# One 512-column matmul on hi|lo activations in place of two of 256, in a split-float32 GEMM chain

## The chip, the core and the metric

The program runs on one core of one Trainium2 chip. The metric is the device time of one execution in microseconds, from the first to the last instruction; the median of several runs is quoted. In this kernel TensorE (PE) multiplies into PSUM, ScalarE (ACT) and VectorE (DVE) read PSUM and SBUF, GpSimd (POOL) works on SBUF, SyncE (SP) issues the weight transfers.

## What is computed

Two transformer-like blocks over 256 tokens of width 2048, all in float32. First block: RMS norm, an input projection, attention over three dilations (8 heads), a diagonal state-space mixer with a gated unit, an output projection, and a gated FFN of 5632. Second block: one wide input projection, a two-way linear recurrence (LRU), local attention, attention over a memory, three gated branches merged and projected, and an FFN of 8192 with squared ReLU.

```
hn = rmsnorm(h, norm1);  q, k, v, u = split(hn @ w_in)
h  = h + concat([attention(q, k, v), ssm(u)]) @ w_out
hn = rmsnorm(h, norm2);  h = h + (silu(hn @ w_gate) * (hn @ w_up)) @ w_down
x  = rmsnorm(h, final)
xr, gr, q, k, v, qm, gl = split(rmsnorm(x, pre) @ w_in_2)
merged = sum over 3 branches of sigmoid(gl_n + b) * (y_n @ w_br_n)
x  = x + rmsnorm(merged @ w_out_2)
x  = x + rmsnorm(relu(rmsnorm(x) @ w_up)^2 @ w_down)
```

Nearly all the work is products of activations [256 x K] with weights [K x N].

## The kernel before

**Numbers.** The matmuls take f32r, which the kernel uses as a float32 of fewer bits. So each operand is split into a high part, its f32r rounding, and a low part, the rest; a product a*w is taken as ah*wh + al*wh + ah*wl, three f32r matmuls into the same PSUM address.

**Tiling.** The activations lie transposed, 128 features x 256 tokens a tile, 16 tiles; XH, XL and UH, UL are the split parts of two operand buffers, each a tensor of its own. A GEMM is a chain of *bodies* (138 in the program); a body has 8 *slots*, and makes 512 output features: slots 0 to 3 are the four quarters of K for the first 256 outputs, slots 4 to 7 for the second 256. A slot is one transfer of weights (512 KB where K is 2048) into RAW, a ring of 4 buffers. In `units` a slot has 2 x kt triples of matmuls (kt is 4, in three stages 2 and in one 3): n picks 128 output features, k the 128 rows of K; each result is 128 x 256 and lies in the first half (0:T) of a bank of 512 floats. Outputs 0 and 1 of the half body p use banks 2p and 2p+1 of `gemm_psum`. In a few stages (`tokens_out`) the activations are the stationary operand and 256 weight columns stream.

**Who feeds whom.** For each slot ScalarE (`upper`, L688) waits for the transfer and for TensorE to have left the ring buffer (mm_done of four slots earlier), and rounds RAW into HI. VectorE (`lower`, L1104) subtracts into LO and counts up lo_done, which TensorE waits for before the slot, and the queue of SyncE before it loads the buffer again. At a half body's first slot TensorE also waits for evac[p], which says that banks 2p and 2p+1 have been read.

**Order.** ScalarE and VectorE both run `stream`: at slot j of a body they first split slot j's weights and then do the *event* of slot j-3 (LAG = 3). The events of slots 3 and 7 hold the evacuation of a finished half body: on VectorE `taken` waits for mm_done and gives the view of the two banks, and the operation that follows (scaling by the norm, an addition to the residual) reads PSUM and counts evac[p]. In the gated unit (glu) ScalarE takes the sigmoid from PSUM itself. The other events are attention, state space, recurrence and so on; their small matmuls stand between TensorE's slots and use the other four banks. What an engine waits for in an event holds back the next slot's split too, because each queue is in order.

The residual stages (`residual`, L1373 in the output projection of the state-space part, L1368 in the last down projection of the first block) have the longest event: VectorE adds, multiplies by the next gain (L1375), waits for ScalarE's rounding into XH, and subtracts into XL (L1377); ScalarE waits for L1375 before it rounds.

## Time and profile before

| | before |
|---|---|
| median of 3 runs | 3399.64 us (3398.23 to 3400.7) |
| span of the profiled execution | 3399.2 us |
| TensorE busy | 3279.3 us, 96% |
| VectorE busy | 2136.7 us, 63% |
| ScalarE busy | 1530.1 us, 45% |
| GpSimd busy | 532.6 us, 16% |
| read from HBM | 571.13 MB |

A busy matmul row is as long as the matmul takes from its start to its modelled end; the next one begins long before that, so a group's busy figure is not its share of the time. The share is to be taken from a stretch without gaps, by the count of its matmuls.

### The profile page before, as it was taken

Reading aid. Unit: us, or ns where it says so; the run is one execution under the profiler, and the core shown is the slowest. Engines: PE = TensorE matmul, PEld = TensorE weight load, DVE = VectorE, ACT = ScalarE, POOL = GpSimd, SP = SyncE. Lnnn points to the kernel's source line nnn. Section 1 sums busy time; section 2 is a strip of 40 time slices with the busy share of each in tenths; the row PEclk is TensorE's granted clock in tenths of the full one; section 3 lists DMA queues with packets and bytes.
Section 4 is the critical chain, followed back from the end, with each engine's and each line's share of the span. In section 5 each row is a group of like instructions: output and inputs, shape, how many; then the busy total and the mean of one; then the engine's idle time right before and its main releaser. Section 6 shows DMA issues by size and latency. Waiting matters only on the chain.

```text
span 3399.2 us, 67239 instructions
## 1 busy us (share of the span) xinstructions
PE 3279.3 (96%) x26280; PEld 3212.2 (94%) x26280; DVE 2136.7 (63%) x2409; ACT 1530.1 (45%) x1885; POOL 532.6 (16%) x511
## 2 busy tenths in 40 slices
PE   5999999999999999899999999999997999999997
PEld 5898889999999999899999999999997999999997
DVE  7788887755555555857865666455556655555555
ACT  3444445454334344337753556444333333333342
POOL 5343443300000000703430000000014000000002
PEclk9999999999999999999999999999998999999999
DMA  6444444655555555555555444555553455555553
GB/s 212 151 154 147 156 142 143 193 184 167 194 184 180 176 182 171 162 193 173 167 195 179 154 149 161 178 174 174 181 173 118 161 186 178 187 180 186 180 185 124
DMA packets 169036, 580.49 MB, mean 171 GB/s; under 512 B 19072, under 2 KB 20864, under 8 KB 168896
## 3 DMA queue, kind: packets, MB, share of 16 engines
q1 hardware_dynamic: 160272, 558.16, 49.8%
q0 software_dynamic: 3408, 10.75, 0.9%
q10 hardware_dynamic: 5216, 9.64, 0.8%
q8 instruction: 97, 1.59, 0.2%
q14 instruction: 43, 0.35, 0.0%
HBM read 571.13 MB, written 7.34 MB: 170 GB/s over the span
## 4 chain that ended last, share of the span: by engine, by line
PE 87%; DVE 9%; issue 2%; ACT 2%; DMA 0%; ACTq 0%; DVEq 0%; POOL 0%; POOLq 0%; SPq 0%
PE gemm_psum L326 26%; PE gemm_psum L327 26%; PE gemm_psum L328 26%; DVE weights_lo L1104 3%; PE gemm_psum L320 1%; PE gemm_psum L321 1%; PE gemm_psum L322 1%; PE bank_b L338 1%; ACT weights_hi L688 1%; DVE projections L1375 0%; DVE x_lo L1127 0%; PE bank_s L570 0%; PE bank_b L591 0%; PE bank_s L602 0%; DVE late L1217 0%
## 5 line engine op out<-in xcount | busy, mean ns | idle before, releaser
L1104 DVE TENSOR_TENSOR weights_lo<-weights,weights_hi 128x1024 fp32r<-128x1024 f32 (+2 forms) x1104 | 1349.9, 1236 | 968.6 <-ACT weights_hi L688 962.6
L688 ACT ACTIVATE weights_hi<-weights 128x1024 fp32r<-128x1024 f32 (+2 forms) x1104 | 1109.9, 1018 | 1427.0 <-PE gemm_psum L328 1262.3
L326 PE MATMUL gemm_psum<-x_hi,weights_hi 128*128 128x256 f32 x5120 | 1467.4, 287 | 68.3 <-DVE weights_lo L1104 41.7
L327 PE MATMUL gemm_psum<-x_lo,weights_hi 128*128 128x256 f32 x5120 | 1455.9, 284 | 0.0
L328 PE MATMUL gemm_psum<-x_hi,weights_lo 128*128 128x256 f32 x5120 | 1455.5, 284 | 0.0
L326 PEld LDWEIGHTS gemm_psum<-x_hi,weights_hi 128*128 128x128 f32 x5120 | 985.2, 192 | 81.0 <-issue 37.4
L327 PEld LDWEIGHTS gemm_psum<-x_lo,weights_hi 128*128 128x128 f32 x5120 | 985.3, 192 | 0.8
L328 PEld LDWEIGHTS gemm_psum<-x_hi,weights_lo 128*128 128x128 f32 x5120 | 985.1, 192 | 0.0
L326 PE MATMUL gemm_psum<-u_hi,weights_hi 128*128 128x256 f32 x2880 | 826.0, 287 | 17.6 <-DVE weights_lo L1104 15.2
L327 PE MATMUL gemm_psum<-u_lo,weights_hi 128*128 128x256 f32 x2880 | 816.2, 283 | 0.0
L328 PE MATMUL gemm_psum<-u_hi,weights_lo 128*128 128x256 f32 x2880 | 816.1, 283 | 0.0
L326 PEld LDWEIGHTS gemm_psum<-u_hi,weights_hi 128*128 128x128 f32 x2880 | 549.2, 191 | 24.1 <-DVE weights_lo L1104 15.8
L327 PEld LDWEIGHTS gemm_psum<-u_lo,weights_hi 128*128 128x128 f32 x2880 | 549.2, 191 | 1.0
L328 PEld LDWEIGHTS gemm_psum<-u_hi,weights_lo 128*128 128x128 f32 x2880 | 549.1, 191 | 0.0
L1886 POOL TENSOR_TENSOR work<-projections 128x512 f32 x16 | 26.4, 1649 | 956.3 <-DVE projections L1696 698.0
L1803 POOL TENSOR_TENSOR work<-projections 128x512 f32<-128x512 f32 x8 | 12.3, 1539 | 711.8 <-DVE projections L1368 711.8
L1872 POOL DMA_DIRECT2D work<-memk_scratch x8 | 4.3, 536 | 500.1 <-ACT late L1002 364.7
L320 PE MATMUL gemm_psum<-weights_hi,u_hi 128*128 128x256 f32 x256 | 75.3, 294 | 0.0
L321 PE MATMUL gemm_psum<-weights_hi,u_lo 128*128 128x256 f32 x256 | 72.4, 283 | 0.0
L322 PE MATMUL gemm_psum<-weights_lo,u_hi 128*128 128x256 f32 x256 | 72.3, 283 | 0.0
L1083 ACT ACTIVATE u_hi<-work 128x512 f32 (+1 forms) x32 | 20.2, 632 | 109.5 <-DVE work L1682 109.5
L1780 POOL TENSOR_TENSOR late<-late 128x256 f32<-128x256 f32 x32 | 31.0, 970 | 154.0 <-DVE late L1221 154.0
(338 smaller groups left out, 2553.6 us busy)
## 6 DMA issues: line engine op xcount, KB each, us to landing
weights<-in_w_branch SPq DMA_DIRECT2D x192, 512.0 KB, 3.3
weights<-in_w_gu SPq DMA_DIRECT2D x176, 512.0 KB, 3.4
weights<-in_w_up SPq DMA_DIRECT2D x128, 512.0 KB, 3.5
weights<-in_w_down SPq DMA_DIRECT2D x128, 512.0 KB, 3.3
weights<-in_w_dn SPq DMA_DIRECT2D x64, 512.0 KB, 3.3
weights<-in_w_in_qk SPq DMA_DIRECT2D x32, 512.0 KB, 3.3
weights<-in_w_mem_k SPq DMA_DIRECT2D x32, 512.0 KB, 3.5
weights<-in_w_mem_v SPq DMA_DIRECT2D x32, 512.0 KB, 3.4
```

Of the source, the lines that this page charges most:

```text
L320: pe.matmul(o, ah, wh, start=first, stop=False)
L321: pe.matmul(o, al, wh, start=False, stop=False)
L322: mm = pe.matmul(o, ah, wl, start=False, stop=end)
L326: pe.matmul(o, wh, xh[:, kk, :], start=first, stop=False)
L327: pe.matmul(o, wh, xl[:, kk, :], start=False, stop=False)
L328: mm = pe.matmul(o, wl, xh[:, kk, :], start=False, stop=end)
L338: mm = pe.matmul(bank_b[:, n, :], b_stage[rows, n, :], u_stage[rows, :], start=True, stop=True)
L688: act.activation(HI[:, j % RING, 0:g.kt * GC], RAW[:, j % RING, 0:g.kt * GC], ACT.Copy)\
L1083: act.activation(UH[:, ix(b(4, 2 * (slot // 4)), 2), :], up_space, ACT.Copy).then_inc(up_hi, 1)
L1104: dve.tensor_tensor(LO[:, j % RING, cols], RAW[:, j % RING, cols], HI[:, j % RING, cols].bitcast(f32), ALU.subtract).then_inc(lo_done, 1)
L1780: pool.tensor_tensor(state_h[:, 0, :], prod_c[:, 0, :], prod_s[:, 1, :], ALU.add)
L1886: pool.tensor_tensor(squares[:, 0:2, :], t, t, ALU.mult).then_inc(sq_step, 1)
```

## The change

HI and LO become the two planes of one tensor WS (`weights_split`), XH and XL those of XS (`x_split`, 512 floats a tile: high | low), UH and UL those of US. In `units` one matmul with the high weights streams both planes of the activations, 512 columns, into the whole bank (`both`); a second, with the low weights, streams the high plane into the first half. In the `tokens_out` stages the high activations stand still and high | low weights stream. So a result now lies in two halves of a bank that must be added.

No VectorE operation reads both halves: ScalarE copies the second half of both banks to SBUF (`staged`, tensor `halves`, one buffer for each p), at the head of the events of slots 3 and 7, after waits for mm_done and for evac[p] of the body before. `taken` on VectorE waits for that copy (half_out) in place of mm_done, adds the first half onto it, counts `summed`, waits for it, and hands on the buffer in SBUF; the operation that used to read PSUM reads SBUF, and counts evac[p] as before. In glu, VectorE makes the sum too and ScalarE's sigmoid waits for it. After the last stage ScalarE does the events that were left over (slots 5 to 7), which it did not need to before.

```
-                            pe.matmul(o, wh, xh[:, kk, :], start=first, stop=False)
-                            pe.matmul(o, wh, xl[:, kk, :], start=False, stop=False)
-                            mm = pe.matmul(o, wl, xh[:, kk, :], start=False, stop=end)
+                            pe.matmul(both, HI[:, j % RING, cols], xs[:, kk, :, :], start=first, stop=False)
+                            mm = pe.matmul(o, LO[:, j % RING, cols], xs[:, kk, 0, :], start=False, stop=end)
...
+            def staged(g, events):
+
+                def f(slot, b):
+                    if slot in (3, 7):
+                        p = slot // 4
+                        wait(act, mm_done, b(SLOTS, SLOTS * g.first + slot + 1))
+                        wait(act, evac[p], b(1, g.first))
+                        act.activation(halves[p], GP[:, 2 * p:2 * p + 2, T:2 * T], ACT.Copy).then_inc(half_out, 1)
+                    events(slot, b)
+                return f
...
             def taken(g, b, slot):
 
-                wait(dve, mm_done, b(SLOTS, SLOTS * g.first + slot + 1))
-                return GP[:, 2 * (slot // 4):2 * (slot // 4) + 2, 0:T]
+                p = slot // 4
+                wait(dve, half_out, b(2, 2 * g.first + p + 1))
+                dve.tensor_tensor(halves[p], halves[p], GP[:, 2 * p:2 * p + 2, 0:T], ALU.add).then_inc(summed, 1)
+                wait(dve, summed, b(2, 2 * g.first + p + 1))
+                return halves[p]
...
-                    act.wait_ge(mm_done, SLOTS * (glu.first + b()) + slot + 1)
+                    act.wait_ge(summed, 2 * (glu.first + b()) + slot // 4 + 1)
...
+            for slot in range(SLOTS - LAG, SLOTS):
+                late[0](slot, late[1])
```

The order of the instructions on TensorE, in the first slot of the program, before:

```order
L326 MATMUL gemm_psum<-x_hi,weights_hi 128x256 [waits lo_done,xl_done]
L327 MATMUL gemm_psum<-x_lo,weights_hi 128x256
L328 MATMUL gemm_psum<-x_hi,weights_lo 128x256
L326 MATMUL gemm_psum<-x_hi,weights_hi 128x256
L327 MATMUL gemm_psum<-x_lo,weights_hi 128x256
L328 MATMUL gemm_psum<-x_hi,weights_lo 128x256
```

and with the change (L326 and L327 are lines of the changed kernel):

```order
L326 MATMUL gemm_psum<-x_split,weights_split 128x512 [waits lo_done,xl_done]
L327 MATMUL gemm_psum<-x_split,weights_split 128x256
L326 MATMUL gemm_psum<-x_split,weights_split 128x512
L327 MATMUL gemm_psum<-x_split,weights_split 128x256
L326 MATMUL gemm_psum<-x_split,weights_split 128x512
```

Each triple has become a pair; nothing else moved there.

On VectorE, the first evacuation of the output projection of the state-space part, before:

```order
L1104 TENSOR_TENSOR weights_lo<-weights,weights_hi 128x512 [waits hi_done] x4
L1373 TENSOR_TENSOR residual<-residual,gemm_psum 128x512 [waits mm_done]
L1375 TENSOR_TENSOR projections<-residual,vecs 128x512 [waits evac0]
L1377 TENSOR_TENSOR x_lo<-projections,x_hi 128x512 [waits res_hi]
L1104 TENSOR_TENSOR weights_lo<-weights,weights_hi 128x512 [waits hi_done]
```

and with the change (L1116 is the weights' low part, L1123 the addition in `taken`, L1390 the residual):

```order
L1116 TENSOR_TENSOR weights_split<-weights,weights_split 128x512 [waits hi_done] x4
L1123 TENSOR_TENSOR halves<-halves,gemm_psum 128x512 [waits half_out]
L1390 TENSOR_TENSOR residual<-residual,halves 128x512 [waits summed]
L1392 TENSOR_TENSOR projections<-residual,vecs 128x512 [waits evac0]
L1394 TENSOR_TENSOR x_split<-projections,x_split 128x2x256 [waits res_hi]
L1116 TENSOR_TENSOR weights_split<-weights,weights_split 128x512 [waits hi_done]
```

One operation more stands ahead of the residual, and two waits, for ScalarE's copy and for the sum.

On ScalarE, at the same place, with the change (before, the row of L697 is not there; L687 rounds the weights, L876 the activations):

```order
L687 ACTIVATE weights_split<-weights 128x512 [waits mm_done,raw_in1]
L687 ACTIVATE weights_split<-weights 128x512 [waits mm_done,raw_in2]
L697 ACTIVATE halves<-gemm_psum 128x512 [waits evac0,mm_done]
L876 ACTIVATE x_split<-projections 128x2x256 [waits res_g]
L687 ACTIVATE weights_split<-weights 128x512 [waits mm_done,raw_in3]
```

The copy stands between the rounding of slot 6's weights and that of slot 7's.

## Rows read from the trace of the kernel before

**Rows 1.** The page: busy time and share, then the granted clock in 40 slices.

```profile
PE 3279.3 (96%) x26280; PEld 3212.2 (94%) x26280; DVE 2136.7 (63%) x2409; ACT 1530.1 (45%) x1885; POOL 532.6 (16%) x511
...
PEclk9999999999999999999999999999998999999999
```

**Rows 2.** The page: the chain that ended last, by line.

```profile
PE gemm_psum L326 26%; PE gemm_psum L327 26%; PE gemm_psum L328 26%; DVE weights_lo L1104 3%; PE gemm_psum L320 1%; PE gemm_psum L321 1%; PE gemm_psum L322 1%; PE bank_b L338 1%; ACT weights_hi L688 1%; DVE projections L1375 0%; DVE x_lo L1127 0%; PE bank_s L570 0%; PE bank_b L591 0%; PE bank_s L602 0%; DVE late L1217 0%
```

**Rows 3.** Groups by line: busy us, mean ns of one, idle time before them.

```profile
L326 PE MATMUL gemm_psum<-x_hi,weights_hi 128*128 128x256 f32 x5120 | 1467.4, 287 | 68.3 <-DVE weights_lo L1104 41.7
L327 PE MATMUL gemm_psum<-x_lo,weights_hi 128*128 128x256 f32 x5120 | 1455.9, 284 | 0.0
...
L326 PE MATMUL gemm_psum<-u_hi,weights_hi 128*128 128x256 f32 x2880 | 826.0, 287 | 17.6 <-DVE weights_lo L1104 15.2
```

**Rows 4.** Stretches: length, busy us (count) of each engine, clock, DMA share, GB/s.

```profile
265.60:394.80 129.20, 125.99 (x900) 113.25 (x899) 107.94 (x142) 61.53 (x86) 51.71 (x54) 0.99 0.47 149
...
601.90:654.80 52.90, 48.04 (x387) 46.44 (x385) 43.04 (x55) 24.27 (x41) 25.99 (x21) 1.00 0.54 169
...
1352.10:1431.30 79.20, 70.85 (x578) 69.43 (x577) 68.24 (x62) 29.52 (x40) 51.49 (x49) 1.00 0.48 155
...
1527.00:1632.90 105.90, 105.90 (x834) 104.23 (x834) 77.00 (x97) 83.94 (x120) 43.66 (x36) 1.00 0.52 169
...
2916.90:3009.00 92.10, 92.10 (x770) 92.10 (x769) 46.04 (x42) 34.38 (x33) 0.00 (x0) 1.00 0.56 183
```

**Rows 5.** Timeline of TensorE: start us, length us, what.

```profile
3000.03 0.28 PE L326 MATMUL gemm_psum<-u_hi,weights_hi 128*128 128x256 f32 x1
3000.04 0.19 PEld L327 LDWEIGHTS gemm_psum<-u_lo,weights_hi 128*128 128x128 f32 x1
3000.15 0.28 PE L327 MATMUL gemm_psum<-u_lo,weights_hi 128*128 128x256 f32 x1
```

**Rows 6.** Chain in order of time, and timeline: other matmuls.

```profile
2123.65 3.46 PE bank_s L602 x16
...
1444.19 0.95 PE L532 MATMUL bank_a<-ones,squares 128*128 128x1 f32 x8
1444.98 0.19 PEld L326 LDWEIGHTS gemm_psum<-x_hi,weights_hi 128*128 128x128 f32 x1
```

**Rows 7.** A stretch at the lower clock, and two matmuls in it.

```profile
2625.70:2628.30 2.60, 2.20 (x11) 1.91 (x9) 2.60 (x3) 1.71 (x4) 2.01 (x1) 0.50 0.00 0
...
2626.21 0.41 PE L328 MATMUL gemm_psum<-x_hi,weights_lo 128*128 128x256 f32 x1
2626.42 0.41 PE L326 MATMUL gemm_psum<-x_hi,weights_hi 128*128 128x256 f32 x1
```

**Rows 8.** Timeline of one slot's two weight splits, in brackets idle before.

```profile
3003.53 1.06 ACT L688 ACTIVATE weights_hi<-weights 128x1024 fp32r<-128x1024 f32 x1 [1.82 <-PE gemm_psum L328]
...
3004.63 1.23 DVE L1104 TENSOR_TENSOR weights_lo<-weights,weights_hi 128x1024 fp32r<-128x1024 f32 x1 [1.66 <-ACT weights_hi L688]
```

**Rows 9.** Timeline of half a body of the state-space output projection.

```profile
626.92 0.39 PE L326 MATMUL gemm_psum<-u_hi,weights_hi 128*128 128x256 f32 x1 [0.51 <-DVE weights_lo L1104]
...
629.13 0.68 DVE L1373 TENSOR_TENSOR residual<-residual,gemm_psum 128x512 f32 x1
629.96 0.69 DVE L1375 TENSOR_TENSOR projections<-residual,vecs 128x512 f32 x1
630.80 0.63 ACT L866 ACTIVATE x_hi<-projections 128x512 f32 x1 [3.71 <-DVE projections L1375]
631.58 0.69 DVE L1377 TENSOR_TENSOR x_lo<-projections,x_hi 128x512 f32 x1 [0.92 <-ACT x_hi L866]
...
633.48 0.38 PE L326 MATMUL gemm_psum<-u_hi,weights_hi 128*128 128x256 f32 x1 [0.55 <-DVE weights_lo L1104]
```

**Rows 10.** Groups by line, shapes kept apart: a PSUM copy, a PSUM addition, a self-wait.

```profile
L776 ACT ACTIVATE work<-bank_s 128x512 f32<-128x512 f32 x8 | 4.6, 580 | 0.0
...
L1696 DVE TENSOR_TENSOR projections<-projections,gemm_psum 128x512 f32 x18 | 12.4, 688 | 12.4 <-PE gemm_psum L328 12.4
...
L1492 DVE SCALAR_TENSOR_TENSOR work<-projections,vecs,work 128x255 f32<-128x255 f32 x16 | 7.8, 484 | 2.4 <-DVE work L1490 2.3
```

More of the change, by code:

```diff
@@ L165, in program @@
         consts = sb("consts", [P, 4])
+        HS = sb("halves", [P, 2, 2 * T])
+        halves = [HS[:, n, :].rearrange("p (a t) -> p a t", a=2) for n in range(2)]
         def vec(name, a=0, n=None):
@@ L250, in program @@
         hi_done, lo_done, mm_done = sem("hi_done"), sem("lo_done"), sem("mm_done")
+        half_out, summed = sem("half_out"), sem("summed")
         angle_in, theta_done, angle_done, bbar_done = sem("angle_in"), sem("theta_done"), sem("angle_done"), sem("bbar_done")
@@ L858, in glu_events @@
                        .then_inc(gh_done, 1)
-            late = stream(act, glu, upper, late, glu_events, tail=gelu_y)
+            late = stream(act, glu, upper, late, staged(glu, glu_events), tail=gelu_y)
             def out_ssm_events(slot, b):
@@ L866, in out_ssm_events @@
                     act.activation(XH[:, ix(tiles, 2), :], ZP[:, 0:2, :], ACT.Copy).then_inc(res_hi, 1)
-            late = stream(act, out_ssm, upper, late, out_ssm_events)
+            late = stream(act, out_ssm, upper, late, staged(out_ssm, out_ssm_events))
             act.wait_ge(ol_done, H1)
@@ L904, in _ @@
             for n, (up, down) in enumerate(ffn1):
-                late = stream(act, up, upper, late, up_events(up, done))
+                late = stream(act, up, upper, late, staged(up, up_events(up, done)))
                 done += up.bodies
-                late = stream(act, down, upper, late, last_down_events if n == 2 else nothing,
+                late = stream(act, down, upper, late, staged(down, last_down_events if n == 2 else nothing),
                               tail=(second_constants, lru_constants, None)[n])
@@ L1061, in branch_events @@
                 return f
-            late = stream(act, branches[0], upper, late, branch_events(0))
-            late = stream(act, branches[1], upper, late, branch_events(1), tail=operand(0, q_late, UH))
-            late = stream(act, branches[2], upper, late, branch_events(2), tail=operand(1, qm, UH))
-            late = stream(act, out2, upper, late, nothing, tail=operand(2, merged, XH))
+            late = stream(act, branches[0], upper, late, staged(branches[0], branch_events(0)))
+            late = stream(act, branches[1], upper, late, staged(branches[1], branch_events(1)), tail=operand(0, q_late, UH))
+            late = stream(act, branches[2], upper, late, staged(branches[2], branch_events(2)), tail=operand(1, qm, UH))
+            late = stream(act, out2, upper, late, staged(out2, nothing), tail=operand(2, merged, XH))
             def mixed():
@@ L1086, in _ @@
             for n, (up, down) in enumerate(ffn2):
-                late = stream(act, up, upper, late, up2_events(8 * n), tail=mixed if n == 0 else None)
-                late = stream(act, down, upper, late, nothing)
+                late = stream(act, up, upper, late, staged(up, up2_events(8 * n)), tail=mixed if n == 0 else None)
+                late = stream(act, down, upper, late, staged(down, nothing))
+            for slot in range(SLOTS - LAG, SLOTS):
+                late[0](slot, late[1])
             root(7, bank_y[:, 0, :], rms[:, 1, :])
@@ L1350, in glu_events @@
             def glu_events(slot, b):
+                if slot in (3, 7):
+                    taken(glu, b, slot)
                 if slot == 7:
```

55 lines of the change are left out of this document (26 added, 29 removed).

## The prediction

> **What bounds the kernel now.** Read the page first. TensorE is busy 96% of a span of 3399.2 us at a mean granted clock of 0.99 of the 2.4 GHz level, and the next engine, VectorE, 63% [rows 1]. The chain that ended last lies on TensorE for 87%, in three lines of equal weight, the three matmuls of one product [rows 2]. The groups by line say what these are: 128x128 weights over 256 columns, a busy figure of 284 to 287 ns each [rows 3]. These overlap, so the price of one is not its row but its share of a stretch. The stretch from 2916.9 to 3009.0 is one down projection of the second block, 4 bodies of 8 slots of 24 matmuls = 768, in 92.1 us: **120.0 ns each**, 2.88 us a slot, with no gap [rows 4]. At 2.4 GHz 256 columns last 106.7 ns, so each matmul pays 13.3 ns on top of its columns. The program has 138 bodies, 1104 slots, and 8448 such triples (5120+2880+256+192 by the counts in the groups by line), together 8448 x 360 ns = 3041 us of the 3399.
>
> The change leaves the columns as they are (512+256 = 3x256) and takes away one instruction, one weight load, of each triple. So the question is what the 13.3 ns belong to: to each matmul, to its weight load, or to its columns.
>
> **The matmuls.** Three places of the trace bear on it. (1) A stream of plain f32 matmuls at 2.4 GHz, 16 records in 3.46 us, 216 ns each [rows 6]: L602 has 8 matmuls there and 16 records, each of which passes its 256 columns twice (512 column times, 213.3 ns) and each has a full weight load of its own. There the extra is 3 ns, and a load is hidden under 512 column times. (2) Where the clock stood at 1.2 GHz (granted 0.50), our own matmuls start 0.21 us apart [rows 7], 256/1.2 = 213 ns: nothing on top. (3) Eight matmuls of a single column, each with a full load: after the first, seven loads between 1444.19 and 1444.98, 0.113 us each [rows 6]. So a load alone repeats in 113 ns, less than our 120, and in our stream the next load starts 0.01 us after the matmul does [rows 5]: it would be through before the 120 ns are over. The load alone does not explain the 13.3 ns; something at the start of each full-rate matmul with a load beside it does, and it vanishes when the columns go at half rate, as in (1) and (2).
>
> I take it as **fixed for each matmul**: the 512-column one costs 213.3+13.3 = 226.7 ns, the pair 346.7 against 360.0, a gain of 13.3 ns a triple. Bounds: 216+120 = 336 ns if the wide matmul behaves as in (1) (gain 24), and 240+120 = 360 if the extra goes with the columns (gain 0). A stream of 512 full-rate columns does not occur before the change, so no row is nearer; the middle value is also the one between the bounds, and (1) and (2) show that what exists is not a share of every column in every mode.
>
> By the Trainium skill ("TensorE: Matmul & The Clock Gate", section "Back-to-back issue gap") a matmul takes its columns over 2.4 GHz plus 2.5 ns; by that the triple would cost 328 and the pair 325 ns, a gain of 3 ns, and the change would lose more than it wins. The trace has 120 ns where that rule gives 109, and agrees with it only in the f32 stream; the time by that rule would fall beside the third rival below.
>
> Two stages don't give this gain, since TensorE waits for VectorE in them: the output projection of the state-space part (601.9 to 654.8, VectorE busy 43.0 of 52.9 us) and the last down projection of the first block (1352.1 to 1431.3, 68.2 of 79.2) [rows 4]. They hold 128 and 192 triples. So 8128 triples x 13.3 ns = **-108 us** (bounds -193 and 0).
>
> **The evacuations.** Each body has two, 276 in all. Added: on ScalarE a copy of 128x512 from PSUM, 0.58 us by the row of the same shape; on VectorE an addition of 128x512 with one operand in PSUM, 0.69 us, and its wait for itself, 0.15 us as where an operation reads what the one before wrote [rows 10]. That is 0.84 us of VectorE and 0.6 of ScalarE each, 232 and 160 us over the run. VectorE's wait is now for half_out, which stands behind ScalarE's split of slot 6 (or 2 of the next body); behind it on VectorE are the event's arithmetic and the low part of the next slot's weights, and TensorE waits for that. What covers it: ScalarE rounds a slot's weights as soon as TensorE has left the ring's buffer, with three slots still to go before that slot. Its row starts at 3003.53, VectorE's low part ends at 3005.86 [rows 8], 2.33 us after the release, and TensorE starts on it three slots = 8.64 us after the release: 6.3 us in hand. With the change three slots last 8.3 us and the chain grows by 0.6+0.84 and less than 1 us of queueing: still over 3 us. **Nothing** in stages of that kind.
>
> Where the cover is thin:
> - The output projection of the state-space part. A half body takes 6.56 us (TensorE's stalls end at 626.92 and 633.48) against 5.76 of matmuls, and VectorE runs through all of it: addition, gain, a wait for ScalarE's high part, low part, four weight splits [rows 9]. The copy can start before VectorE comes (the matmuls of slot 7 end at about 628.4, VectorE adds at 629.13), so only VectorE's own 0.84 us counts: 8 x 0.84 = **+7 us** (up to 8 x 1.45 = 12).
> - The last down projection of the first block has the same shape and less lead: 8 x (0.84 to 1.45) = **+9 us** (7 to 12).
> - Where a stage can't start before the last evacuation of the one before (into the first block's FFN, into the second block, into its MLP, and the end) the chain grows by 0.6+0.84 = 1.45 us: 4 x 1.45 = **+6 us**.
> - The recurrent stages (ScalarE 83.9 and VectorE 77.0 of 105.9 us) and the state-space stages before 577 (VectorE 107.9 of 129.2, 84%) [rows 4]. A body of 32.3 us there has 27.0 of VectorE's work; it becomes 28.7 of 31.4 us (91%) and stays under TensorE's time, but chains through both engines are long. Nothing at best, 60 us if a third of the added VectorE time there shows; I take **+15 us**.
>
> Sum on the profiled execution: 3399.2 - 108 + 7 + 9 + 6 + 15 = 3328. The span lies 0.4 us under the median of the runs, 3399.64, which is inside their own spread (3398.2 to 3400.7). **Forecast 3330 us.**
>
> **The rivals.**
> - *The weight load is what binds* 256-column matmuls, and a wide one hides it: 336 ns a pair. For it: the load alone already takes 113 of the 120 ns, and the f32 stream pays 3 ns. Against: the next load's row starts with the matmul's own. The gain is 193 us, and as TensorE outruns the splits sooner I take 40 for the costs: 3245 us. The Trainium skill gives a load its columns over 1.2 GHz (same page, section "LDWEIGHTS"), 107 ns for 128 columns, which would put the 256-column matmul right at that edge; the trace agrees within 6 ns.
> - *Half fixed, half by columns*: 233+120 = 353 ns, a gain of 6.7 x 8128 = 54 us; 3399 - 54 + 37 = 3382 us.
> - *By columns alone*, the slower side: reading 4-byte columns at 2.4 GHz is what falls short, 240 ns for 512. For it: the extra is absent exactly where columns go at half rate. Then the gain is 0 and the 37 us of evacuations stay: 3436 us. It decides from a wide matmul of 235.5 ns on, where 8128 x 4.6 ns just pay the 37.
> - *The evacuations hurt more*: the two halves run through three engines in order, and in the state-space and recurrent stages VectorE becomes the bound. With the fixed price, -108 + 22 + 60 = 3373 us.
>
> **How the numbers follow.** Fixed price 0.42, load-bound 0.14, half and half 0.18, by columns 0.18, costly evacuations 0.08. The range from 3240 to 3408 leaves out the case by columns and little else. A measurement of this kernel can tell about 0.2% (7 us) from no change. Faster by more than that: 0.40 + 0.14 + 0.13 + 0.06 = 0.73; within it 0.07; slower 0.20.
>
> **What would show it.** In a down projection of the second block, a slot of 8 pairs: 2.77 us if fixed, 2.69 if load-bound, 2.88 if by columns (92.1 us for the stage becomes 88.7, 86.1 or stays). Copy rows of some 0.58 us x276 on ScalarE and additions of 0.69 us x276 on VectorE. In the two VectorE-bound stages, 60 and 88 us instead of 52.9 and 79.2. TensorE's waits for weights_lo outside these and the stage starts should stay near zero; if they spread over the state-space stages, my 15 us are too few. The forecast is wrong in kind if the slot stays at 2.88 us.

## The result, and the profile after

The changed kernel takes **3420.76 us** (median of 6 runs, 3407.51 to 3430.6) against 3399.18 (6 runs, 3397.82 to 3400.7): ratio 1.006, 95% interval 1.0042 to 1.0078. That is 21.6 us slower, where 3330 was forecast and 3240 to 3408 was the range. The profiled execution is one of 3427.63 us with a span of 3425.9.

The page of the changed kernel: busy time, and the chain that ended last by line.

```profile
PE 3237.2 (94%) x17832; PEld 2763.8 (81%) x17832; DVE 2312.3 (67%) x2685; ACT 1672.8 (49%) x2161; POOL 534.8 (16%) x511
...
PE 77%; DVE 14%; ACT 5%; issue 3%; ACTq 0%; DVEq 0%; DMA 0%; POOL 0%; POOLq 0%; SPq 0%
```

8448 matmuls and their loads are gone, and TensorE's busy time fell by only 42 us (3279.3 in [rows 1]). 10 points of the chain have moved from TensorE to VectorE, ScalarE and issue (it was 87% TensorE): TensorE waits more. Its waits for the weights' low parts grew from 56.9 us in all to 93.4.

Groups of the changed kernel, by line (busy us, mean ns of one, idle before them):

```profile
L326 PE MATMUL gemm_psum<-x_split,weights_split 128*128 128x512 f32 x5120 | 1837.9, 402 | 88.0 <-DVE weights_split L1116 61.1
L327 PE MATMUL gemm_psum<-x_split,weights_split 128*128 128x256 f32 x5120 | 1444.7, 282 | 0.0
...
L697 ACT ACTIVATE halves<-gemm_psum 128x512 f32<-128x512 f32 x276 | 164.9, 597 | 522.9 <-PE gemm_psum L327 504.8
L1123 DVE TENSOR_TENSOR halves<-halves,gemm_psum 128x512 f32<-128x512 f32 x276 | 189.2, 686 | 274.9 <-ACT halves L697 273.6
```

They answer to [rows 3]. The copy (597 ns) and the addition (686 ns) are what their nearest rows said. New are the two idle figures: ScalarE stands 523 us, summed over 276 copies, until the matmuls of the slot are done, and VectorE 275 us until the copy is. Not all of that is added idle time: before the weights' rounding ScalarE stood 1427 us and now stands 925. It waits at another place in its queue.

Stretches of the changed kernel (length; busy us of TensorE, its loads, VectorE, ScalarE, GpSimd; clock; DMA): one of the two long attention stages over the memory, the output projection of the state-space part, the last down projection of the first block, the first of two recurrent stages, and a down projection of the second block.

```profile
393.30:523.70 130.40, 121.97 (x643) 96.65 (x642) 111.89 (x152) 64.26 (x94) 52.71 (x54) 1.00 0.42 137
610.70:677.50 66.80, 52.83 (x259) 43.70 (x257) 49.08 (x63) 29.46 (x51) 26.15 (x21) 0.90 0.46 140
1359.10:1446.50 87.40, 72.65 (x387) 61.66 (x386) 74.05 (x70) 34.59 (x49) 51.44 (x49) 0.95 0.44 141
1543.50:1659.30 115.80, 107.69 (x579) 92.44 (x577) 82.86 (x104) 85.28 (x127) 41.68 (x36) 0.97 0.48 154
2950.30:3040.80 90.50, 90.50 (x515) 78.44 (x514) 50.93 (x50) 38.35 (x41) 0.00 (x0) 1.00 0.59 190
```

Against [rows 4] the last came down from 92.1 to 90.5 us, not to 88.7; its 256 pairs have no gap, 353 ns a pair. The other stages grew: 52.9 to 66.8, 79.2 to 87.4, 105.9 to 115.8.

But 353 ns is not the price everywhere. Four rows of TensorE's timeline; from the first to the second, and from the third to the fourth, it is 50 pairs:

```profile
1200.33 0.39 PE L326 MATMUL gemm_psum<-u_split,weights_split 128*128 128x512 f32 x1
...
1217.66 0.39 PE L326 MATMUL gemm_psum<-u_split,weights_split 128*128 128x512 f32 x1
...
3050.32 0.40 PE L326 MATMUL gemm_psum<-x_split,weights_split 128*128 128x512 f32 x1
...
3067.99 0.40 PE L326 MATMUL gemm_psum<-x_split,weights_split 128*128 128x512 f32 x1
```

The earlier 50 take 17.33 us, **346.6 ns a pair**, the forecast price; the later 50 take 17.67, **353.4 ns**. Each pace holds for hundreds of microseconds, until TensorE waits or runs matmuls of another shape; then it may change. Over all places of this trace where four matmuls of the GEMM follow without a wait at 2.4 GHz the mean is 350.8 ns.

### The profile page after: what moved, and what is told of

Read it like the earlier page. It is cut to its first block, busy times and chain, and to the rows that moved or that the text cites. A ratio compares the mean times of both kernels' runs of the same rounds, so it can differ in the third digit from the quotient of the medians.

```text
span 3425.9 us, 51477 instructions
## 1 busy us (share of the span) xinstructions
PE 3237.2 (94%) x17832; PEld 2763.8 (81%) x17832; DVE 2312.3 (67%) x2685; ACT 1672.8 (49%) x2161; POOL 534.8 (16%) x511
## 3 DMA queue, kind: packets, MB, share of 16 engines
q0 software_dynamic: 3408, 10.75, 1.0%
## 4 chain that ended last, share of the span: by engine, by line
PE 77%; DVE 14%; ACT 5%; issue 3%; ACTq 0%; DVEq 0%; DMA 0%; POOL 0%; POOLq 0%; SPq 0%
PE gemm_psum L326 47%; PE gemm_psum L327 24%; DVE weights_split L1116 4%; PE gemm_psum L322 2%; ACT weights_split L687 1%; DVE halves L1123 1%; PE gemm_psum L323 1%; DVE late L1232 1%; ACT halves L697 1%; PE bank_s L601 0%; PE bank_b L337 0%; DVE projections L1392 0%; PE bank_b L590 0%; ACT work L955 0%; DVE x_split L1684 0%
## 5 line engine op out<-in xcount | busy, mean ns | idle before, releaser
L326 PE MATMUL gemm_psum<-x_split,weights_split 128*128 128x512 f32 x5120 | 1837.9, 402 | 88.0 <-DVE weights_split L1116 61.1
L1116 DVE TENSOR_TENSOR weights_split<-weights,weights_split 128x1024 fp32r<-128x1024 f32 (+2 forms) x1104 | 1341.7, 1235 | 652.8 <-ACT weights_split L687 649.5
L687 ACT ACTIVATE weights_split<-weights 128x1024 fp32r<-128x1024 f32 (+2 forms) x1104 | 1105.0, 1017 | 925.2 <-PE gemm_psum L327 791.9
L327 PE MATMUL gemm_psum<-x_split,weights_split 128*128 128x256 f32 x5120 | 1444.7, 282 | 0.0
L326 PEld LDWEIGHTS gemm_psum<-x_split,weights_split 128*128 128x128 f32 x5120 | 973.3, 190 | 337.4 <-issue 49.3
L326 PE MATMUL gemm_psum<-u_split,weights_split 128*128 128x512 f32 x2880 | 1038.1, 404 | 36.2 <-DVE weights_split L1116 32.3
L327 PEld LDWEIGHTS gemm_psum<-x_split,weights_split 128*128 128x128 f32 x5120 | 979.0, 191 | 0.8
L327 PE MATMUL gemm_psum<-u_split,weights_split 128*128 128x256 f32 x2880 | 812.8, 282 | 0.0
L326 PEld LDWEIGHTS gemm_psum<-u_split,weights_split 128*128 128x128 f32 x2880 | 547.4, 190 | 174.5 <-DVE weights_split L1116 30.0
L327 PEld LDWEIGHTS gemm_psum<-u_split,weights_split 128*128 128x128 f32 x2880 | 550.3, 191 | 0.9
L697 ACT ACTIVATE halves<-gemm_psum 128x512 f32<-128x512 f32 x276 | 164.9, 597 | 522.9 <-PE gemm_psum L327 504.8
L1123 DVE TENSOR_TENSOR halves<-halves,gemm_psum 128x512 f32<-128x512 f32 x276 | 189.2, 686 | 274.9 <-ACT halves L697 273.6
L1820 POOL TENSOR_TENSOR work<-projections 128x512 f32<-128x512 f32 x8 | 12.3, 1541 | 704.9 <-DVE projections L1385 704.9
```

The costliest lines, as they stand in the source:

```text
L326: pe.matmul(both, HI[:, j % RING, cols], xs[:, kk, :, :], start=first, stop=False)
L327: mm = pe.matmul(o, LO[:, j % RING, cols], xs[:, kk, 0, :], start=False, stop=end)
L687: act.activation(HI[:, j % RING, 0:g.kt * GC], RAW[:, j % RING, 0:g.kt * GC], ACT.Copy)\
L697: act.activation(halves[p], GP[:, 2 * p:2 * p + 2, T:2 * T], ACT.Copy).then_inc(half_out, 1)
L1116: dve.tensor_tensor(LO[:, j % RING, cols], RAW[:, j % RING, cols], HI[:, j % RING, cols].bitcast(f32), ALU.subtract).then_inc(lo_done, 1)
L1123: dve.tensor_tensor(halves[p], halves[p], GP[:, 2 * p:2 * p + 2, 0:T], ALU.add).then_inc(summed, 1)
```

## The experiments

All ratios are against runs of the kernel before on the same chip. Times of two experiments are often of two chips, but the kernel before had medians of 3399.1 to 3399.8 us on those with several runs, so differences of a few us can be read. First the two halves of the change, each alone.

**e1_wide_only.** The changed kernel without copy and addition:

```
             def staged(g, events):
+                return events
...
             def taken(g, b, slot):
-                wait(dve, half_out, ...); dve.tensor_tensor(halves[p], halves[p], GP[..., 0:T], ALU.add)...
-                return halves[p]
+                wait(dve, mm_done, b(SLOTS, SLOTS * g.first + slot + 1))
+                return GP[:, 2 * p:2 * p + 2, 0:T]
```

> TensorE runs the wide pairs, everything else is as in the kernel before: no copy of the second half by ScalarE, no addition, the evacuation reads the first half alone. Left out of the computation: the low part times the high part (the second half of each bank), which is never added. This isolates what the wide matmuls give. My theory now (a wide matmul costs 236 ns and the pair 353 ns, as the records of the changed kernel show in quiet stages): 7 ns less for each of 8128 to 8448 pairs, 57 us, so 3399 - 57 = 3342 us, and out_ssm, down2, lru_gate, in_q2 and the recurrent stages are each no longer than before. Rival 1 (the price on record, 346.7 ns; the copies and additions of the changed kernel stretch its wide matmuls from 227 to 236 ns by contention): 3399 - 108 = 3291 us, a stage of 256 pairs 88.7 us instead of the 90.4 of the changed kernel. Rival 2 (the weight split, which now has 7 ns less a pair to hide in, is itself the new bound of the loaded stages): 3370 us or more, with lru_gate and in_q2 still some 10 us longer than before.

Measured: 3324.72 us (3322.98 to 3336.41), ratio 0.9788 (0.9774 to 0.9802): **75 us faster**, between my theory and rival 1. Its stretches: the same down projection, the state-space output projection, the recurrent stage.

```profile
2857.50:2946.30 88.80, 88.80 (x515) 77.66 (x514) 46.00 (x42) 34.35 (x33) 0.00 (x0) 1.00 0.59 191
592.60:645.70 53.10, 47.05 (x258) 38.96 (x257) 43.05 (x55) 24.26 (x42) 26.26 (x21) 1.00 0.52 169
1501.10:1604.90 103.80, 103.51 (x579) 89.78 (x577) 75.51 (x96) 82.20 (x120) 43.67 (x36) 1.00 0.53 172
```

The down projection takes the 88.7 us of the fixed price. Earlier stages of the same trace run at 353 ns (the second up projection of the first block takes 180.9 us, in the changed kernel too). So contention with the copies is not what makes 353: they don't exist here. Rival 2 falls as well: the recurrent stage is 2.1 us shorter than before.

**e2_three_summed.** The changed kernel with three 256-column matmuls:

```
-        pe.matmul(both, HI[:, j % RING, cols], xs[:, kk, :, :], start=first, stop=False)
+        pe.matmul(o, HI[:, j % RING, cols], xs[:, kk, 0, :], start=first, stop=False)
+        pe.matmul(GP[:, 2 * p + n, T:2 * T], HI[:, j % RING, cols], xs[:, kk, 1, :], start=False, stop=False)
```

> The opposite half of the change: three 256-column matmuls again, but with the low-times-high product in the second half of the bank, and with the copy by ScalarE and the addition by VectorE as in the changed kernel. This isolates what the new evacuation costs. My theory (the copy and the addition cost where VectorE or ScalarE is what TensorE waits for, and nothing in quiet stages): about 3399 + 70 = 3470 us, between 3450 and 3490; out_ssm some 66 us, down2 87, lru_gate and in_q2 some 8 us longer than before, quiet stages 92.1 us as before. Rival (the evacuation is as cheap as the record says, 37 us in all, and the rest is the matmuls' price): 3436 us.

Measured: 3483.75 us (3479.29 to 3486.24), ratio 1.0248 (1.0234 to 1.0262): the evacuation costs **84 us**, not 37. Stretches: memory attention, state-space output projection, recurrent stage, down projection of the second block.

```profile
398.80:529.80 131.00, 124.46 (x899) 112.00 (x898) 112.20 (x152) 64.28 (x94) 52.91 (x53) 1.00 0.42 137
615.60:678.80 63.20, 49.73 (x387) 47.93 (x385) 49.00 (x63) 29.36 (x50) 26.15 (x21) 0.97 0.48 148
1567.60:1681.70 114.10, 108.39 (x835) 104.28 (x833) 86.20 (x104) 85.09 (x127) 41.89 (x36) 1.00 0.49 157
2997.10:3089.30 92.20, 92.20 (x771) 92.20 (x770) 50.91 (x50) 38.32 (x41) 0.00 (x0) 1.00 0.56 187
```

The last line is as before: where TensorE is alone the bound, copy and addition are free, as forecast. -74.7 and +84.4 make +10; the change made +22. The traces, by the table further down, say where such a rest lies (21 us there, since the profiled run of the changed kernel was 7 us over its median). 14 us are in the stages before 577, the gated unit and state-space output, the recurrent stages and the first two branches: there the two halves together cost more than their sum. The other 7 fit the pace: the mean pair was 349.6 ns in e1's trace and 350.8 in the other, 1.2 x 8448 = 10 us over all stages.

**e3_hybrid.** Wide pairs where they didn't lose:

```
+    for g in (in_u, in_qk, in_v, in_k2, in_v2, in_qm, branches[2], out2, up0, down0, up1, down1, up2) + last FFN:
+        g.wide = True
...
+                            if not g.wide:
+                                (the three matmuls of before; no copy, no addition)
```

> Wide pairs, copy and addition only in the stages that came out no longer in the changed kernel: in_u, in_qk, in_v, in_k2, in_v2, in_qm, branch 2, out2, up0, down0, up1, down1, up2 and the eight stages of the last feed-forward part; triples and the old evacuation in memory, out_attn, glu, out_ssm, down2, lru_in, lru_gate, in_q2, branches 0 and 1. My theory (gain and cost are both local to their stage): the sum of the better of the two stage lengths, 3399 - 40 = 3359 us, between 3345 and 3375, faster than both. Rival 1 (the costs are not local: what the addition delays on VectorE, and low clock after new waits, comes back in whichever stage is next loaded): 3380 to 3400 us. Rival 2 (the matmuls' gain is only in the one profiled run): 3399 us.

Measured: 3363.17 us (3355.68 to 3369.53), ratio 0.99 (0.9885 to 0.9915). My theory: the memory, recurrent and first two branch stages have their old lengths to 0.1 us. Gain and cost are local to their stage.

**e4_streams** and **e5_orders** measure matmuls with nothing beside them, behind the last down projection.

```
+            def stream_of(n_cols, count, out_cols=P, ...):
+                for i in range(count):
+                    pe.matmul(bank[0:out_cols, 0:n_cols], HI[...out_cols], UH[...n_cols], start=True, stop=True)
+            stream_of(256, 60); stream_of(512, 60); stream_of(384, 60); ...
```

> The kernel before with eight streams of matmuls on TensorE put in behind its last down-projection, while the other engines are quiet: 60 each of 256, 512, 384 and 320 columns, 60 of 512 and of 256 columns with a weight tile of 32 columns instead of 128, 30 of 512 columns in plain float32, and 30 pairs of 512 and 256. They measure the price of one matmul against its columns without any evacuation or traffic. My theory (extra half by columns, half fixed): 120, 236, 178 and 149 ns, the pair 356, the short weight tile changes nothing. Rival 1 (13.3 ns fixed for each matmul, and contention in the changed kernel): 120, 227, 173 and 147 ns, pair 347. Rival 2 (by columns alone): 120, 240, 180, 150. Rival 3 (bound by the load of the weights at 256 columns): the short tile at 256 columns falls to some 107 ns.

First and last row of 50 matmuls of 512 columns:

```profile
3385.72 0.39 PE L663 MATMUL bank_b<-u_hi,weights_hi 128*128 128x512 f32 x1
...
3397.05 0.39 PE L663 MATMUL bank_s<-u_hi,weights_hi 128*128 128x512 f32 x1
```

11.33 us, **226.7 ns each**. Over 50 matmuls likewise 120.0 at 256 columns, 146.7 at 320, 173.3 at 384: columns over 2.4 GHz plus 13.3 ns every time. Rival 1, which was the forecast's price, and not the theory I held by then. The last stream, 512 and 256 in turn, took its 347 ns a pair too (346.7). Rival 3 had one point: with weights of 32 columns a 256-column matmul took 113.3 ns, half way to its 107. But a 512-column one took 231.6, more than with full weights. So the size of the load matters a little; as every matmul here has a load of its own, the streams don't tell whether the 13.3 ns belong to the matmul or to its load.

```
+            for order in ((512, 256), (512, 512, 256, 256), (512,) * 4 + (256,) * 4):
+                for k in range(8):
+                    apart(5 + k)                 # matmuls of 128 columns
+                    for i in range(64): one(order[i % len(order)], ...)
```

> The kernel before with 24 streams of 64 matmuls behind its last down-projection, no traffic and no evacuation beside them: 8 streams that alternate 512 and 256 columns, 8 in the order 512, 512, 256, 256, 8 in the order four of 512, four of 256; ahead of each stream stand 5 to 12 matmuls of 128 columns. In the changed kernel a pair costs 346.7 ns in some stretches and 353.3 ns in others, and keeps its pace until TensorE is interrupted. Theory 1 (the pace is a matter of how a 512 and a 256 fall behind each other when a burst begins, without any other engine): some of the 8 alternating streams run at 346.7 and some at 353.3 ns a pair, and where same sizes stand together the price is 346.7 or nearly so for all. Theory 2 (the slow pace comes from the traffic of the other engines): all 24 streams run at 346.7 ns a pair.

The alternating streams with 6 and with 9 matmuls ahead; from each first row to its last it is 23 pairs.

```profile
3392.32 0.40 PE L660 MATMUL bank_a<-u_hi,weights_hi 128*128 128x512 f32 x1
...
3400.45 0.40 PE L660 MATMUL bank_s<-u_hi,weights_hi 128*128 128x512 f32 x1
...
3428.66 0.39 PE L660 MATMUL bank_a<-u_hi,weights_hi 128*128 128x512 f32 x1
...
3436.63 0.39 PE L660 MATMUL bank_s<-u_hi,weights_hi 128*128 128x512 f32 x1
```

8.13 and 7.97 us: 353.5 and 346.5 ns a pair. Of the 8 alternating streams 5 ran at 353.3 and 3 at 346.7; two and two gave 348.3 to 348.6 in all 8, four and four 350.8 in all 8. Theory 1 in its main part: the pace arises in TensorE, from two sizes in turn, without any other engine. Its other part, same sizes together at nearly 346.7, fell with the 350.8.

**e11_lead_in** asks what picks the pace (edit as in e5, other lists of orders and lead-ins).

> Again streams of 64 matmuls behind the last down-projection of the kernel before: 12 that alternate 512 and 256 columns, six of them with 5 matmuls of 128 columns ahead and six with 8, then 4 streams (5, 6, 7, 8 ahead) of each of three orders: 256 first and alternating, three of 512 and three of 256, eight of 512 and eight of 256. Theory 1 (the lead-in decides which of the two paces an alternating stream takes, 5 ahead gave 353.3 ns a pair and 8 ahead 346.7): six at 353.3 and six at 346.7. Theory 2 (the moment of the start against something that runs on its own decides): the six with the same lead-in are not all alike. Three and three should lie between two and two (348.3) and four and four (350.8), some 350 ns; eight and eight, with few changes of size, near 346.7 if each change costs, or at 350 or more if long runs of 256 columns cost.

Five ahead: the first at 353.3, the other five at 346.7. Eight ahead: all six at 353.3, although e5's stream with eight ahead ran at 346.7. So the lead-in alone does not decide, and theory 1 falls. Nor did each stream draw by itself: in each six all but at most the first are alike. That would fit a pace set by what ran before, which these runs don't show. 256 first: 346.7 to 346.9 in 4 of 4. Three and three 350.0, eight and eight 349.2, between the two values expected for it.

**In the kernel: e6_grouped, e9_twos, e12_small_first.** The same pairs in another order within a slot.

```
e6:  for step in range(2 * g.kt):  k, low = step % g.kt, step >= g.kt
e9:  steps = [(n, k, low) for a in range(0, len(pieces), 2) for low in (False, True) for n, k in pieces[a:a + 2]]
e12: steps = [(n, k, low) for n, k in pieces for low in ((False, True) if j % UNITS == 0 and k == 0 else (True, False))]
```

> The changed kernel with one thing altered: of each 4 (or 3, 2) pairs that go to one half bank the wide matmuls are issued first, then the 256-column ones, instead of alternately. Same work, same evacuation. Theory 1 (the slow pace belongs to the alternation of sizes): the stretches at 353.3 ns a pair go, mean 347 instead of 350.8, 8448 x 3.8 ns = 32 us less on TensorE, some of it lost where other engines bind: 3420 - 25 = 3395 us, between 3385 and 3405. Theory 2 (the pace comes from elsewhere): 3407 to 3431 us as the changed kernel, stretches at 353.3 stay.

3423.05 us (3421.87 to 3428.4), ratio 1.0069 (1.0055 to 1.0082). I had taken 347 ns for this order. By the streams' 350.8, which is also the changed kernel's mean, no gain was due, and none came.

> The changed kernel with the matmuls of a slot in the order wide, wide, small, small (two pairs of k together) instead of alternately. Same work, same evacuation. The streams without any other engine gave 346.7 or 353.3 ns a pair for the alternate order, 350.8 for four and four, 348.3 for two and two, always. Theory 1 (the pace of a pair is made in TensorE by the order of sizes alone): stages of 256 pairs at 89.2 us, the time 2.5 ns x 8448 = 21 us under the order of four and four (3423 us), 3402 us, between 3396 and 3408, and the spread of the runs, 23 us for the changed kernel and 6.5 us for four and four, stays small. Theory 2 (in the kernel other things decide, and 3423 is the changed kernel's own level): 3418 to 3425 us.

3406.96 us (11 runs, 3402.64 to 3408.85), ratio 1.002 (1.0011 to 1.0029): 16 us under e6 where 21 were expected, inside the range of theory 1. Down projection of the second block in e6, in e9 and in e12:

```profile
2954.20:3044.00 89.80, 89.80 (x514) 78.47 (x513) 50.92 (x50) 38.35 (x41) 0.00 (x0) 1.00 0.58 190
```

```profile
2933.30:3022.50 89.20, 89.20 (x515) 77.83 (x514) 50.85 (x50) 38.34 (x41) 0.00 (x0) 1.00 0.57 194
```

```profile
2891.90:2982.20 90.30, 90.30 (x513) 78.48 (x512) 50.92 (x50) 38.34 (x41) 0.00 (x0) 1.00 0.61 190
```

By 256 pairs 351, 348 and 353 ns, for the first two what the streams gave. From the first FFN on, the other undisturbed stages of wide pairs in these traces run at the same three values, while the alternate order changes between 346.7 and 353.3 from stage to stage. The spread of the runs is 6.5 us in e6 and 6.2 in e9, against 23 for the alternate order; that fits a pace drawn anew in each run, but only one run of each kernel has a trace.

> The hybrid of 22 stages with wide pairs again, now with the 256-column matmul of each pair ahead of the wide one (but for the first pair of each half bank, which has to open it with the wide one). So sizes alternate, with one small-small and one wide-wide neighbourhood in each group. In the streams an alternation that began with 256 columns ran at 346.7 ns a pair in 4 of 4, one that began with 512 in 8 of 20. Theory 1 (a burst that begins with the small matmul takes the fast pace, and most slots here begin so): 347 ns a pair, 1.6 ns x 5632 = 9 us under the order of two and two (3349 us): 3340 us, between 3335 and 3346. Theory 2 (the start decides nothing of itself, each interruption and each change of bank draws anew): a mean between 346.7 and 353.3, 3345 to 3365 us, with a spread over 8 us.

3369.35 us (3368.73 to 3370.24), ratio 0.9913 (0.99 to 0.9927), 20 us over the same hybrid in twos. Both theories fall: 256 first ran at the dear pace here, 353 ns in the whole trace, and a spread of 1.5 us over 5 runs says that the others did too. Why the kernel differs from the streams (each group has one small-small and one wide-wide neighbourhood, and the accumulation differs) wasn't tried.

**e10_hybrid_twos**: e3 with e9's order.

> The hybrid (wide pairs, copy and addition in 22 stages where TensorE waits for nothing, triples and the old evacuation elsewhere; 3363 us) with the order wide, wide, small, small in its wide stages. The hybrid's wide stages ran at a mean of 349.7 ns a pair in its profiled run. Theory 1 (pace by order, gain and cost local): 348.3 ns a pair on 5632 wide pairs, 8 us less: 3355 us, between 3350 and 3360, with a spread under 8 us instead of 14. Theory 2: 3355 to 3370 us with the old spread.

**3348.91 us** (3347.59 to 3349.55), ratio 0.985 (0.9836 to 0.9863), the fastest complete version: 50 us under the kernel before, 72 under the changed one, and 1 us below the expected range: the order in twos gave 14 us here instead of 8. The 8 were worked out from e3's profiled run, which was its fastest, 3355.68 us: against that one it is 7. Its down projection, state-space output projection and recurrent stage:

```profile
2877.90:2967.10 89.20, 89.20 (x515) 77.83 (x514) 50.85 (x50) 38.38 (x41) 0.00 (x0) 1.00 0.61 191
598.80:652.00 53.20, 48.03 (x386) 46.44 (x385) 43.08 (x55) 24.30 (x41) 26.30 (x21) 1.00 0.54 172
1506.80:1612.70 105.90, 105.90 (x834) 104.23 (x833) 76.97 (x97) 83.93 (x120) 43.66 (x36) 1.00 0.52 170
```

**e7_add_only, e8_copy_and_wait**: which part of the evacuation costs. Both from e2.

```
e7:  staged(g, events) returns events (no copy);  in taken:
-                wait(dve, half_out, ...); dve.tensor_tensor(halves[p], halves[p], GP[..., 0:T], ALU.add)
+                wait(dve, mm_done, ...);  dve.tensor_tensor(halves[p], zeros, GP[..., 0:T], ALU.add)
e8:  in taken:
                 wait(dve, half_out, b(2, 2 * g.first + p + 1))
-                dve.tensor_tensor(...).then_inc(summed, 1); wait(dve, summed, ...); return halves[p]
+                return GP[:, 2 * p:2 * p + 2, 0:T]
```

> Three 256-column matmuls as in the run with halves summed (3483.8 us), but ScalarE's copy is taken away: VectorE adds a tile of zeros to the first half as soon as the matmuls are done, and waits for its own sum. Left out of the computation: the second half of the bank (low times high) is never added. What is left is the additions alone. Theory 1 (VectorE's own time is what costs: about 0.69 + 0.1 us at each of 276 places, in front of the weight split): most of the 84 us stays, 3450 to 3470 us. Theory 2 (waiting for ScalarE is what costs, since its queue brings the copy late): only some 25 us stay, 3415 to 3435 us.

3440.79 us (3440.02 to 3441.72), ratio 1.0119 (1.0104 to 1.0135).

> The opposite: ScalarE copies the second half, VectorE waits for the copy but adds nothing and reads the first half from the bank as before. Left out of the computation: low times high. Theory 1 (VectorE's own time costs): 3410 to 3430 us. Theory 2 (the wait for ScalarE costs): 3440 to 3465 us. The two runs together should come to about 84 us above the kernel before if the costs add up.

3441.0 us (3437.98 to 3442.95), ratio 1.0121 (1.0105 to 1.0136). Each costs 41 us, together 82 of the 84, so the two costs add up as expected. e7 lies between the ranges of its two theories, e8 at the lower edge of theory 2's (3440 to 3465): half and half, but in different stages. Memory attention and recurrent stage in e7:

```profile
398.20:529.20 131.00, 124.46 (x899) 112.00 (x897) 112.20 (x153) 59.50 (x86) 52.88 (x53) 1.00 0.42 137
1557.90:1663.80 105.90, 105.90 (x834) 104.24 (x833) 86.78 (x104) 82.79 (x120) 41.88 (x36) 1.00 0.53 169
```

and in e8:

```profile
395.00:521.20 126.20, 124.35 (x899) 112.04 (x898) 106.79 (x144) 64.27 (x94) 52.69 (x53) 1.00 0.44 142
1538.30:1651.60 113.30, 107.62 (x835) 104.56 (x833) 76.33 (x96) 85.02 (x127) 40.55 (x36) 1.00 0.48 158
```

In the memory stage (126.2 us before) the additions do all of it, 131.0; in the recurrent stage (105.9) the copy and the wait for it, 113.3. Change of the stage lengths in us, by the first GEMM matmul of each, and for the end by the last one of all:

| stages | before | e1 | e2 | e7 | e8 | changed |
|---|---|---|---|---|---|---|
| input, memory, attention output (to 577) | 549.4 | -7.8 | +11.6 | +11.2 | +1.2 | +6.9 |
| glu, state-space output | 77.1 | -0.1 | +12.3 | +8.0 | +6.0 | +17.1 |
| first FFN but its last down | 697.3 | -14.0 | +5.4 | +4.2 | +4.0 | -15.6 |
| its last down | 79.2 | -0.2 | +8.0 | +6.7 | +0.6 | +8.2 |
| second block's first input stage | 95.6 | -2.6 | +3.2 | +1.4 | +0.3 | +1.3 |
| two recurrent stages | 211.8 | -2.5 | +16.5 | +1.0 | +14.9 | +17.8 |
| k, v, memory query | 140.1 | -3.4 | +0.1 | 0.0 | +0.1 | -2.4 |
| first two branches | 440.9 | -9.4 | +18.4 | +6.2 | +9.9 | +11.5 |
| third branch, output | 302.6 | -8.0 | +3.1 | +2.1 | +2.1 | -6.7 |
| last FFN, 8 stages | 755.1 | -27.2 | +1.6 | -0.2 | -0.2 | -11.9 |
| all | 3349.3 | -75.3 | +80.2 | +40.7 | +39.0 | +26.3 |

**e13_copy_last** asks why the copy costs in the recurrent stages. ScalarE's timeline there, at the same place of the kernel before and of e8 (in brackets the idle time before an operation and what ended it):

```profile
1562.27 1.06 ACT L688 ACTIVATE weights_hi<-weights 128x1024 fp32r<-128x1024 f32 x1 [1.38 <-PE gemm_psum L328]
1564.08 1.28 ACT L937 ACT_TABLE_LOAD   x1 [0.76 <-PE bank_s L520]
```

```profile
1575.43 1.06 ACT L689 ACTIVATE weights_split<-weights 128x1024 fp32r<-128x1024 f32 x1 [0.46 <-PE gemm_psum L329]
1581.75 0.60 ACT L699 ACTIVATE halves<-gemm_psum 128x512 f32<-128x512 f32 x1 [5.26 <-PE gemm_psum L329]
1582.36 1.28 ACT L949 ACT_TABLE_LOAD   x1
```

Before, ScalarE split slot 6's weights and went on 0.76 us later with the gate activations. Now it stands 5.26 us at the copy, because slot 3's matmuls are not done, and the activations and the next split stand behind it.

```
             def staged(g, events, copy_last=False):
                 def f(slot, b):
+                    if copy_last:
+                        events(slot, b)
                     (the copy)
+                    if not copy_last:
                         events(slot, b)
...  copy_last=True for lru_gate and in_q2, from e2
```

> The run with three 256-column matmuls and halves summed (3483.8 us; lru_gate 114.1 us, in_q2 114.3 us, before 105.9 each), with one change in these two stages only: ScalarE does the stage's own work of a slot first and the copy of the second half behind it. Theory 1 (ScalarE's queue is what costs: the copy waits 5 us for its slot's matmuls, and the gate activations and weight splits behind it wait with it): the two stages fall to some 108 us each, 3483.8 - 12 = 3472 us, between 3466 and 3476. Theory 2 (VectorE's wait for the copy is what costs): the copy lands up to 4.7 us later behind the activations, VectorE's low parts with it, the two stages grow to 118 us or more, 3490 us or more.

3471.3 us (3464.84 to 3471.59), ratio 1.0203 (1.019 to 1.0217), 12 us under e2. The two recurrent stages:

```profile
1569.70:1676.30 106.60, 106.29 (x834) 104.19 (x834) 86.25 (x104) 85.76 (x127) 41.91 (x36) 1.00 0.51 167
1676.40:1784.40 108.00, 107.15 (x834) 104.17 (x833) 95.95 (x113) 83.51 (x127) 47.26 (x38) 1.00 0.53 171
```

Theory 1: 114.1 and 114.3 fell to 106.6 and 108.0, though the copy comes later. So 13.7 of the 16.5 us were ScalarE's queue. TensorE's waits for low parts in these stages say the same: none before, 10.5 us in e2, 1.2 here. e13 moved the copy in these two stages alone; whether ScalarE's queue is also what costs in the branches and the state-space output was not tried.

## Why the prediction was wrong, point by point

- **The price of one matmul: right.** 13.3 ns come with each matmul and its full weight load (e4: 120.0, 146.7, 173.3, 226.7 ns), not with its columns. The rivals load-bound (336 ns a pair) and by columns (360) are out as prices. The loads of the single-column matmuls start 111 ns apart in the trace, not 113, on which nothing hangs. That the load has no part in the 13.3 ns is not shown: with 32-column weights the extra is 6.7 ns at 256 columns and 18.3 at 512.
- **The price of the pair: the step that failed first.** I added 226.7 and 120.0 as if prices of two sizes could be summed. In alternation they can cost 346.7 or 353.3 (e5), and the changed kernel had both. The number of the half-and-half rival turned up, but its mechanism is refuted. The term of -108 us measured -75 (e1). At that trace's mean of 349.6 ns all 8448 pairs give -88; the 12 or 13 us between are missing mostly in stages where the other engines are loaded, in the two that I had left out and in others (the recurrent stages gave 2.5 us of 6).
- **Output projection of the state-space part, +7 (to 12): too small.** It measured +10.3 in e2, inside the bound, and +13.9 in the changed kernel. The granted clock there is 0.90 against 1.00 [rows 4]. In this stage e13 has the same instructions as e2, three 256-column matmuls, and its trace has the 66.4 us and the 0.90 of the changed kernel (63.2 us at 0.97 in e2):

```profile
616.70:683.10 66.40, 54.02 (x387) 52.20 (x385) 49.10 (x63) 29.43 (x50) 26.21 (x21) 0.90 0.47 142
```

So the 3 us between go with the clock and not with the wide matmuls. I had counted VectorE's 0.84 us alone, since the copy can start early; e8 shows the wait for it at +5.4.
- **Last down projection, +9: right**, +8.0 in e2 and +8.2 in the changed kernel, most of it by the additions (e7 +6.7).
- **Stage boundaries, +6: too small**, and too few were listed. The down projections of the first FFN, the first stage of the second block, the third branch with the output projection, and the last FFN make 5.4 + 3.2 + 3.1 + 1.6 = 13 us in e2. The kind was right: some 10 us into each of the first two down projections TensorE waits once, 1.4 and 2.3 us before, 2.8 and 3.6 in e2.
- **Recurrent and state-space stages, +15: the largest miss.** They make 11.6 + 2.0 (glu) + 16.5 = 30 us in e2, and the first two branches, which had no term at all, 18 more. In those two branches TensorE's waits went from 1.1 us to 12.3, all before the small attention matmuls. The upper bound was also worked out wrongly: all of the added VectorE time in the stages named, some 28 bodies x 2 x 0.84, is 47 us, so a third of it is 16 and not 60; the 15 that I took is that third. For the additions the view was the right one, VectorE near its bound (e7: +11 before 577). For ScalarE I counted the copy's duration and VectorE's wait, and wrote of less than 1 us of queueing. I did not ask what the wait for mm_done holds back on ScalarE's own queue: 5.3 us at one copy in the recurrent stage (e8), 13.7 of the 16.5 us (e13).
- **Nothing in quiet stages: right.** e2's down projection takes 92.2 us as before.

In sum -75 + 84 for -108 + 37. Either error alone would have left it faster: 3399 - 108 + 84 = 3375, 3399 - 75 + 37 = 3361. The rival on the slower side had the right sign for the wrong reason; the costly-evacuations rival named VectorE and should have named ScalarE's queue too, with 84 us.

Left open: why TensorE's two paces exist and what picks one, what part of the branches' 18 us is ScalarE's queue, and how much of the evacuation's cost in all comes through the lower clock behind new waits (3 us in one stage by e2 and e13).

## What to carry to other kernels

When a wait is added at the head of an engine's events, price what is queued behind it on that engine, not the instruction it guards. Here a 0.6 us copy held ScalarE up for 5 us, and 12 us came back when it went behind the other work. A trade of matmuls against evacuation pays where TensorE alone is the bound and loses where it isn't: apply it by stage (3363 us against 3421 everywhere, and 3349 with the pairs in twos). And the price of a mix of matmul sizes has to be measured in the order in which it will run.

## What the runs showed of the hardware

- f32r matmuls with full 128x128 weights, each with a load of its own, cost their columns at 2.4 GHz plus 13.3 ns, at 256, 320, 384 and 512 columns (e4). With weights of 32 columns a 256-column matmul costs less, 113.3 ns, and a 512-column one more, 231.6 (11.58 us for 50; e4).

```profile
3418.58 0.40 PE L663 MATMUL bank_b<-u_hi,weights_hi 128*32 128x512 f32 x1
...
3430.16 0.40 PE L663 MATMUL bank_s<-u_hi,weights_hi 128*32 128x512 f32 x1
```

- Plain f32 of 512 columns has records 429.2 ns apart, two for a matmul (e4): 1024 column times and 2.5 ns. That is the 2.5 ns which the Trainium skill ("TensorE: Matmul & The Clock Gate", section "Back-to-back issue gap") adds to the columns of each matmul, in what it calls the isolated gap; for f32r the measured 13.3 ns stand against it.
- Alternating 512 and 256 columns settles at 346.7 or 353.3 ns a pair and stays there (with 512 first 9 and 12 of 21 streams of e4, e5 and e11); two and two gives 348.3 to 348.6, three and three 350.0, four and four 350.8, eight and eight 349.2.
